# Hybrid RWKV-7 / MoBA / MoE layer: group norm from a centred V inside the attention's loop, probabilities divided by their sums ahead of the turn

## The reference, cut to what matters

```python
# RWKV-7 branch, 8 heads of 64: state recurrence over tokens, then per head and token
sa = einsum('bhij,bhj->bhi', state, a_t)
state = state * w_t + sa[..., None] * b_t + v_t[..., None] * k_t
y_t = einsum('bhij,bhj->bhi', state, r_t)
...
mean = jnp.mean(y, axis=-1); var = jnp.mean(jnp.square(y - mean), axis=-1)
yn = (y - mean) * lax.rsqrt(var + LN_X_EPS) * lnx_g + lnx_b
bonus = jnp.sum(r * k * r_k, axis=-1) * v
out_a = (yn + bonus) * g
# attention branch, 8 heads of 64, here equal to causal attention over 512 tokens
q, k = rope(rms_norm(q)), rope(rms_norm(k))
p = softmax(q @ k.T * 64 ** -0.5 + mask); out_b = p @ v
# merge
merged = sigmoid(g_a) * (out_a @ w_br_rwkv) + sigmoid(g_b) * (out_b @ w_br_moba)
x = x + gate1 * (merged @ w_out)
```

## Time and profile before

| | us |
|---|---|
| median of three runs | 1057.08 |
| the profiled execution | 1062.92 |
| its span | 1061.0 |
| TensorE busy in the span | 1019.7 (96%) |
| Vector engine busy | 532.0 (50%) |
| ScalarE busy | 314.6 (30%) |
| POOL busy | 133.2 (13%) |
| mean granted TensorE clock | 0.995 of full |

### The profile page before, as it was taken

How to read it: one execution, slowest core, us unless ns; L and a number is a source line. 1 busy time by engine, 2 the same in 40 slices (tenths; PEclk the granted TensorE clock), 3 DMA queues, 4 the chain that set the end, 5 groups by cost and what they waited for, 6 DMA issues and landing times.

```text
span 1061.0 us, 19592 instructions
## 1 busy us (share of the span) xinstructions
PE 1019.7 (96%) x8618; PEld 663.9 (63%) x8618; DVE 532.0 (50%) x789; ACT 314.6 (30%) x546; POOL 133.2 (13%) x156
## 2 busy tenths in 40 slices
PE   8999999999898999999999999999999999999998
PEld 6777899999895778878788434444434434344343
DVE  4668842256547656575665524443334334343344
ACT  4467742033336761321333111111111111111110
POOL 0000000464945700000000100000000000000000
PEclk9999999999999999999999999999999999999999
DMA  9632021000003057467488899999999999999994
GB/s 388 230 116 113 3 80 43 12 5 5 4 4 159 8 178 241 156 219 237 168 363 335 305 409 419 428 425 427 427 426 426 427 426 428 428 425 419 415 415 158
DMA packets 42982, 273.29 MB, mean 258 GB/s; under 512 B 8032, under 2 KB 8176, under 8 KB 28688
## 3 DMA queue, kind: packets, MB, share of 16 engines
q1 hardware_dynamic: 39488, 264.42, 62.0%
q0 software_dynamic: 2400, 4.28, 1.2%
q10 hardware_dynamic: 1008, 3.31, 0.8%
HBM read 272.00 MB, written 4.19 MB: 260 GB/s over the span
## 4 chain that ended last, share of the span: by engine, by line
PE 80%; DMA 9%; DVE 5%; ACT 4%; issue 2%; SPq 0%; DVEq 0%; ACTq 0%; POOLq 0%
PE banks L1704 29%; PE banks L2198 18%; PE banks L2212 9%; DMA w_qkv<-in_w 4%; DMA w_tok<-in_w 3%; PE banks L2236 2%; DMA ring<-in_w_mix 2%; PE banks L2237 2%; PE banks L2204 2%; PE banks L2184 1%; PE banks L1864 1%; PE banks L1862 1%; PE banks L1877 1%; ACT xT L913 1%; DVE tokm_r L1084 1%
## 5 line engine op out<-in xcount | busy, mean ns | idle before, releaser
L1583 DVE TENSOR_TENSOR hid<-banks,silu_a 64x512 f32<-64x512 f32 x32 | 22.2, 693 | 197.8 <-ACT silu_a L918 197.8
L2212 PE MATMUL banks<-w_ring,hidT 128*64 128x512 f32 x512 | 116.8, 598 | 1.1 <-ACT hidT L922 1.1
L1570 DVE SCALAR_TENSOR_TENSOR mod<-banks,row_weight,mod 64x512 f32<-64x512 f32 x64 | 47.9, 748 | 70.3 <-PE banks L2212 69.3
L918 ACT ACTIVATE silu_a<-banks 64x512 f32<-64x512 f32 x32 | 18.9, 591 | 206.3 <-PE banks L2199 206.3
L2198 PE MATMUL banks<-w_tok,xT 128*64 128x512 f32 x176 | 78.3, 595 | 0.3 <-DMA w_ring<-in_w 0.3
L2199 PE MATMUL banks<-w_ring,xT 128*64 128x512 f32 x176 | 78.3, 596 | 0.0
L1577 DVE TENSOR_TENSOR x<-x,banks 128x1024 f32<-128x1024 f32 x60 | 71.8, 1219 | 12.6 <-PE banks L2237 12.2
L2199 PE MATMUL banks<-w_tok,xT 128*64 128x512 f32 x176 | 77.9, 595 | 0.0
L2212 PEld LDWEIGHTS banks<-w_ring,hidT 128*64 128x64 f32 x512 | 34.3, 136 | 67.1 <-issue 65.8
L1704 PE MATMUL banks<-x_r,ring_r 128*128 128x512 f32 x192 | 75.0, 391 | 0.6 <-DVE tokm_r L1084 0.6
L2198 PE MATMUL banks<-w_ab,xT 128*64 128x512 f32 x160 | 70.7, 595 | 3.7 <-DMA w_tok<-in_w 3.7
(11 more groups left out here) (394 smaller groups left out, 2314.5 us busy)
## 6 DMA issues: line engine op xcount, KB each, us to landing
w_ring<-in_w SPq DMA_DIRECT2D x42, 2048.0 KB, 25.3
w_tok<-in_w SPq DMA_DIRECT2D x16, 2048.0 KB, 26.2
ada_buf<-in_w_ada SPq DMA_DIRECT2D x64, 256.0 KB, 3.5
w_ab<-in_w SPq DMA_DIRECT2D x8, 2048.0 KB, 25.8
w_qkv<-in_w SPq DMA_DIRECT2D x7, 2048.0 KB, 29.5
w_tok<-in_w SPq DMA_DIRECT2D x24, 512.0 KB, 16.5
w_ring<-in_w SPq DMA_DIRECT2D x24, 512.0 KB, 17.0
w_ring<-in_w SPq DMA_DIRECT2D x10, 1024.0 KB, 15.1
```

Of the source, the lines that this page charges most:

```text
L1570: dve.scalar_tensor_tensor(dst[:, 512 * n:512 * n + 512], bank[5][SLOTS * n:SLOTS * n + SLOTS, :], weight_of(e), gate2[:, n, :], ALU.mult, ...
L1583: dve.tensor_tensor(hid[:, :], bank[3][SLOTS:P, :], silu_a[:, :], ALU.mult).then_inc(hid_v, 1)
L2212: mm = pe.matmul(bank[5][SLOTS * n:SLOTS * n + SLOTS, :], hidT[:, k, :], w2[:, k, 512 * n:512 * n + 512], start=(k == 0), stop=(k == 3))
```

## The change

- A constant "centre" (identity minus the head mean) is added, and turn() makes V's rows with a product with it in place of a transpose. y comes out centred, so the head sums of y and the subtraction go.
- ScalarE squares y from PSUM beside its copy. Four products with 32 columns of `head_ones` put the sums of squares of all four tiles into one bank, ScalarE takes one root of it, the Vector engine one reciprocal in two halves. spread_inverse(ct), two products by 512 columns, spreads a tile's rows over its channels again; normed(ct) on the Vector engine multiplies y with lnx_g and this. lnx_b is added to the bonus by POOL beforehand, so POOL has four passes a tile.
- q and k are turned in the order of the head pairs: four sets before the loop, four in it (units 3 to 6). Gate products 0 and 1 come ahead of the loop, 2 and 3 in units 0 and 7, the spreads in units 1, 2, 8, 9.
- The probabilities are scaled by the inverse sum on the Vector engine (normalised(u)) before turn_probs(u), which now waits for that; the spreading of the inverse sums, its copy and its product go. PROB has three buffers. TensorE's order is scores(u+2), turn_probs(u), weighted(u-1); the Vector engine's is row_max(u+2), normalised(u), y_att(u-1); ScalarE is one unit further ahead with exps.
- The cuts of the branch weights move to units 10 to 13.

```diff
+    parts["centre"] = eye - same / HD
...
+        gn_rows, gn_inverse = mod[:, 0, :], mod[:, 1, :]
+        PROB = [flat[:, at:at + 1024].rearrange("p (o n) -> p o n", o=2) for at in (4096, 5120, 0)]
+        y_squares = ada_buf[:, 1:5, :]
+        QK_ORDER = (0, 4, 1, 5, 2, 6, 3, 7)
+        QK_BANK = (4, 6, 5, 7, 7, 7, 7, 7)
+        QK_AT = {3: 4, 4: 5, 5: 6, 6: 7}
+        GATE_BANK = (4, 5, 7, 7)
+        GATE_AT = {0: 2, 7: 3}
+        SPREAD_GN_AT = {1: 0, 2: 1, 8: 2, 9: 3}
-        BR_CUT_AT = (4, 6, 8, 10)
+        BR_CUT_AT = (10, 11, 12, 13)
...
 ScalarE
+                    act.activation(y_squares[:, :, CH * at:CH * at + CH], bank[2 * n + 1][:, 0:256].rearrange("p (c t) -> p c t", c=CT), ACT.Square)
                     act.activation(ahat[:, :, CH * at:CH * at + CH], ..., ACT.Copy).then_inc(out_a, 1)
+            for i in range(3):
+                turned_qk(i)
+            act.wait_ge(gn_mm, GN_MM["squares"])
+            act.activation(gn_rows, bank[3][:, :], ACT.Sqrt, bias=eps_x, scale=1.0 / HD).then_inc(gn_a, 1)
+            turned_qk(3)
+            act.activation(small[:, 57:58], one, ACT.Exp)
...
             exps(0)
+            gate_out(0)
+            gate_out(1)
+            exps(1)
             for u in range(NUNIT):
-                if u + 1 < NUNIT:
-                    exps(u + 1)
+                if u + 2 < NUNIT:
+                    exps(u + 2)
                 turned_probs(u)
-                if u:
-                    sums_out(u - 1)
+                if u in GATE_AT:
+                    gate_out(GATE_AT[u])
+                if u in QK_AT:
+                    turned_qk(QK_AT[u])
...
 POOL
             for ct in range(CT):
-                seq(pool.tensor_tensor(y_, y_, xs[ct], ALU.mult))
-                seq(pool.tensor_scalar(y_, y_, col["lnx_g"][:, c1], col["lnx_b"][:, c1], ALU.mult, ALU.add))
+                pool.wait_ge(gn_v, 2 + ct + 1)
+                pool.wait_ge(gn_a, 1 + ct + 1)
                 seq(pool.tensor_tensor(y_, y_, zr[:, 8 + ct, :], ALU.add))
...
 Vector engine
+            def norm_inverse(half):
+                c = slice(256 * half, 256 * half + 256)
+                dve.wait_ge(gn_a, 1)
+                dve.reciprocal(gn_inverse[:, c], gn_rows[:, c]).then_inc(gn_v, 1)
+            def normed(ct):
+                dve.wait_ge(gn_mm, GN_MM[f"spread{ct}"])
+                dve.scalar_tensor_tensor(ahat[:, ct, :], ahat[:, ct, :], col["lnx_g"][:, ct:ct + 1], bank[7][:, :], ALU.mult, ALU.mult).then_inc(gn_v, 1)
+            def normalised(u):
+                at, n = 8 * (u % 4), P * (tile_of(u) + 1)
                 dve.wait_ge(exp_a, 2 * u + 2)
-                dve.reciprocal(stat[:, at + 6:at + 8], stat[:, at + 4:at + 6]).then_inc(rsum_v, 1)
+                seq(dve.reciprocal(stat[:, at + 6:at + 8], stat[:, at + 4:at + 6]))
+                for odd in range(2):
+                    prob = PROB[u % 3][:, odd, 0:n]
+                    dve.tensor_scalar(prob, prob, stat[:, at + 6 + odd:at + 7 + odd], None, ALU.mult).then_inc(rsum_v, 1)
...
+            row_max(0)
             norm_inverse(0)
+            row_max(1)
             norm_inverse(1)
-            row_max(0)
-            row_max(1)
             for u in range(NUNIT):
-                inverse_sum(u)
                 if u + 2 < NUNIT:
                     row_max(u + 2)
-                if u in NORM_AT:
-                    norm_inverse(2 + NORM_AT.index(u))
+                normalised(u)
                 if u - 1 in BR_CUT_AT:
                     cut_branch_weights(0, BR_CUT_AT.index(u - 1))
                 if u:
                     y_att(u - 1)
+                if u in SPREAD_GN_AT:
+                    normed(SPREAD_GN_AT[u])
...
 TensorE
-                for i, src in enumerate((zr[:, 8 + ct, :], xp[1], xp[4], ahat[:, ct, :])):
+                pe.matmul(bank[7][:, 0:P], zr[:, 8 + ct, P * t:P * t + P], const("centre"), start=True, stop=True)
+                for i, src in ((1, xp[1]), (2, xp[4]), (3, ahat[:, ct, :])):
...
+            turn_qk(0)
+            turn_qk(1)
+            pe.wait_ge(out_a, NCH - 1)
+            turn_qk(2)
             pe.wait_ge(out_a, NCH)
             for ct in range(CT):
+                mm = pe.matmul(bank[3][32 * ct:32 * ct + 32, :], const("head_ones")[:, 48:80], y_squares[:, ct, :], start=True, stop=True)
+            mm.then_inc(gn_mm, 1)
+            turn_qk(3)
...
             def turn_probs(u):
-                pe.wait_ge(exp_a, 2 * u + 2)
+                pe.wait_ge(rsum_v, 2 * u + 2)
...
             scores(0)
+            pe.wait_ge(gn_a, 1)
             scores(1)
+            pe.wait_ge(s_lora_w, 48)
+            output_gate(0)
+            pe.wait_ge(qk_a, 3)
+            output_gate(1)
+            pe.wait_ge(gn_a, 3)
             for u in range(NUNIT):
-                turn_probs(u)
                 if u + 2 < NUNIT:
                     scores(u + 2)
+                turn_probs(u)
                 if u:
                     weighted(u - 1)
+                (u = 0: output_gate(2); 1, 2: spread_inverse(0), (1); 3 to 6: turn_qk(4) to (7); 7: output_gate(3); 8, 9: spread_inverse(2), (3))
```

More of the change, by code:

```diff
@@ L766, in _, with turned_qk @@
[L766 to L775, removed]
+            def turned_qk(i):
+                j = QK_ORDER[i]
+                act.wait_ge(qk_mm, i + 1)
+                act.activation((qT, kT)[j // 4][:, j % 4, :], bank[QK_BANK[i]][:, :], ACT.Copy, scale=(1.0 if j // 4 else -HD ** -0.5)).then_inc(qk_a, 1)
@@ L1973, in _, with turn_qk, output_gate @@
                         outputs(1, n)
+            def turn_qk(i):
+                j = QK_ORDER[i]
+                c0 = W * (j // 4) + P * (j % 4)
+                for t in range(TT):
+                    if i < 2:
+                        pe.wait_ge(rope_done, 2 * t + 1 + j // 4)
+                    mm = pe.transpose(bank[QK_BANK[i]][:, P * t:P * t + P], qkv[:, t, c0:c0 + P], ident)
+                mm.then_inc(qk_mm, 1)
+            def output_gate(ct):
+                pe.matmul(bank[GATE_BANK[ct]][:, :], lora_g[:, P * ct:P * ct + P], zr[:, 13, :], start=True, stop=True).then_inc(gn_mm, 1)
@@ L1975, in _, with spread_inverse @@
+            def spread_inverse(ct):
+                rows = slice(HD * (ct // 2), HD * (ct // 2) + HD)
+                for h in range(2):
+                    c = 32 * ct + 16 * h
+                    mm = pe.matmul(bank[7][HD * h:HD * h + HD, :], ident[rows, c:c + 1].to_broadcast([HD, HD]), gn_inverse[rows, :], start=True, stop=True)
+                mm.then_inc(gn_mm, 1)
[3 more added lines that the diff above has]
+            turn_qk(2)
             pe.wait_ge(out_a, NCH)
@@ L1976, in _ @@
             for ct in range(CT):
-                pe.matmul(bank[ct][:, :], const("head_ones"), ahat[:, ct, :], start=True, stop=True).then_inc(gn_mm, 1)
-            pe.wait_ge(s_lora_w, 48)
-            for ct in range(CT):
-                pe.matmul(bank[4 + ct][:, :], lora_g[:, P * ct:P * ct + P], zr[:, 13, :], start=True, stop=True).then_inc(gn_mm, 1)
-            for ct in range(CT):
-                pe.wait_ge(gn_v, CT + ct + 1)
-                pe.matmul(bank[ct][:, :], const("head_ones"), xs[ct], start=True, stop=True).then_inc(gn_mm, 1)
@@ L1986, in _ @@
-            for j in range(8):
-                if j >= 4:
-                    pe.wait_ge(qk_a, j - 3)
-                else:
-                    pe.wait_ge(gn_a, j + 1)
-                for t in range(TT):
-                    if j in (0, 4):
-                        pe.wait_ge(rope_done, 2 * t + 1 + j // 4)
-                    c0 = W * (j // 4) + P * (j % 4)
-                    mm = pe.transpose(bank[4 + j % 4][:, P * t:P * t + P], qkv[:, t, c0:c0 + P], ident)
-                mm.then_inc(qk_mm, 1)
@@ L2027, in weighted @@
                 p, i = u // TT, tile_of(u)
-                pe.wait_ge(rsum_v, u + 1)
-                if u:
-                    pe.wait_ge(rs_out, u)
-                for odd in range(2):
-                    at = 8 * (u % 4) + 6 + odd
-                    mm = pe.matmul(bank[7][HD * odd:HD * odd + HD, 0:P], stat[:, at:at + 1].to_broadcast([P, HD]), ident, start=True, stop=True)
-                mm.then_inc(rs_mm, 1)
                 pe.wait_ge(pt_a, u + 1)
```

84 lines of the change are left out of this document (49 added, 35 removed).

## The result

| | before | after |
|---|---|---|
| median | 1056.91 us (1056.73 to 1061.21, 4 runs) | 1106.32 us (1105.23 to 1107.97, 4 runs) |
| the profiled execution, its span | 1062.92, 1061.0 | 1106.41, 1104.6 |
| from scores(2) to the merge's first product | 338.06 to 380.52: 42.5 | 325.99 to 422.31: 96.3 |
| granted clock in that stretch | 0.96 | 0.66 |

The ratio is 1.0434, 95% interval 1.0402 to 1.0466. The forecast was 1078 with a range to 1096: sign and place were right, the size was not.

The account below looks back on a forecast made before the run. The attention was taken as bound by TensorE. Terms -12.9 + 25.6 - 0.4 + 2.5 = +14.8, with +6 for the clock about +21, gave 1084 profiled; with the median 5.8 lower, 1078, range 1065 to 1096.

Parts of the forecast that it names:

- Centring: In 16 turn() calls, one of four turns becomes a product with the constant "centre": +2.5 us, low end +1.8.
- Ahead of the loop: Between recurrence and attention, head sums, sums of squares and half the gate products leave the path: scores(2) earlier, -12.9 us.
- The loop at full clock: Attention loop: TensorE and Vector engine take turns, and moved products add in series: 68.1 against 42.46 us, +25.6.
- scaling's mean far from 0.33: Sign of being wrong: the probability scalings in the loop, priced 0.43 to 0.23 us by width, average far from 0.33.
- TensorE's clock: In the loop, a pause per unit, one in three followed by a clock fall, five falls: +6 us.
- The rule cited there: A matmul engine idling briefly between groups has its clock swing; by it the clock is low in much of the loop.
- the clock stays low: Rival: half clock over three quarters of TensorE's 41 us in the loop, +30 in place of +6: 1102; chance 0.12.
- POOL and the Vector engine: Rival: they slow each other, the fast scaling is lost in half of the units: +2.6 us, inside the range.
- Behind the loop: After the loop, cut_item(0) starts without the last sums_out and the gate products lose most of their wait: -0.4 us.

Follow-up runs that it names:

- e3: The kernel before with only V's turn made a product with the centring constant, head sums and subtraction kept: 1063.4 us, ratio 1.0015.
- e9: The changed kernel with POOL's group-norm passes put behind the attention loop and six identity products in TensorE's pause ahead of each turn: 1113.2 us, ratio 1.0477.
- e6: The changed kernel with POOL's group-norm passes put behind the whole attention loop: 1134.9 us, ratio 1.0711.
- e2: The changed kernel with six products of the identity put into TensorE's pause ahead of each turn_probs(u): 1087.1 us, ratio 1.0232.
- e5: The changed kernel with the Vector engine dividing unit u+1, not u, behind the row maximum of unit u+2: 1065.2 us, ratio 1.0032.
- e8: The changed kernel with the division one unit ahead and written as a tensor_tensor in place of tensor_scalar: 1064.8 us, ratio 1.0022.
- e1: The changed kernel with normalised(u) ahead of row_max(u+2) on the Vector engine: 1085.5 us, ratio 1.0210.
- e13: e11 with the group norm's two reciprocals moved, one behind the row maxima of units 0 and 1, one behind normalised(1): 1058.8 us, ratio 0.9971.
- e11: e5 with POOL's memset of mod put behind the last unit: 1061.6 us, ratio 0.9994.

## Why the prediction was right and wrong

In spans: forecast 1061.0 + 20.8 = 1081.8, measured 1104.6, so 22.8 short. By its steps:

- *Centring*, +2.5: trace 1.8, e3 +2 within its interval. Right.
- *Ahead of the loop*: with the centring, scores(2) at 338.06 + 2.5 - 12.9 = 327.7; it started at 325.99, so 1.7 better.
- *The loop at full clock*, 68.1: the alternation came as described, and e9 has it at 71.9 with neither low clock nor POOL. Of the 3.8 more, 0.8 are the added products that outlast a pause; the rest was not assigned. Right within that. Only the divisions were sized too short even without POOL: the forecast's "scaling's mean far from 0.33" as a sign of being wrong came true, with 0.50 us over the four widths in the change and 0.38 in e9.
- *TensorE's clock*, +6: **this is the step that failed**, by 11: it measures 17.2 us (e6 to e9; 16.8 from the change to e2). Both are what filling the pauses gives back. The forecast counted falls, one for three pauses and 1.7 us each, from pauses that stood alone among busy stretches. In this loop the pauses follow one another, and the granted clock stays at its lower level, 1.2 GHz, for 28 us and more. The rule cited there (the Trainium skill, TensorE: Matmul & The Clock Gate, A second HAM failure mode: psum-queue depth-cycling) was set aside for the count of nine single pauses. Now the trace agrees with it: granted 0.66 over 96 us, and 0.98 to 1.00 once the pauses hold work. The rival "the clock stays low" had the right mechanism, at a chance of 0.12. That its 1102 comes near 1106 is partly luck: it put the clock at 30 us where 17 were measured, and left out POOL's 7.
- *POOL and the Vector engine*, left out of the sum and put at 2.6 as a rival: 7.3 to 7.7 us. The rival took away only the fast form of the division, 0.69 us in place of 0.43; but a pair that meets POOL's passes grew by 0.3 to 1.3 us in the change, and by 3.3 around the memset in e5. The trace of before had the sign of it, unread: of its four cuts of the branch weights, a Vector pass with two inputs in SBUF, the two that start inside a POOL pass are longer (1.67 and 1.53) than the two that don't (1.22, the fourth at 371.78 in the earlier trace rows). The Vector engine's timeline of before, then POOL's:

```profile
353.88 1.67 DVE L1341 TENSOR_TENSOR ring_r<-ring,mid_r 128x1024 fp32r<-128x1024 f32 x1
361.37 1.53 DVE L1341 TENSOR_TENSOR ring_r<-ring,mid_r 128x1024 fp32r<-128x1024 f32 x1
365.61 1.22 DVE L1341 TENSOR_TENSOR ring_r<-ring,mid_r 128x1024 fp32r<-128x1024 f32 x1
```
```profile
353.21 1.26 POOL L987 TENSOR_TENSOR ahat<-ahat,mod 128x512 f32<-128x512 f32 x1
354.57 1.62 POOL L988 TENSOR_SCALAR ahat<-ahat,cols 128x512 f32<-128x512 f32 x1
...
360.55 1.27 POOL L992 TENSOR_TENSOR mid_r<-ahat,zr_r 128x512 fp32r<-128x512 f32 x1
361.88 3.53 POOL L994 MEMSET mod<- 128x4096 f32 x1
```

The first cut ends 1.08 us behind the pass at 353.21, the second 1.08 behind the pass at 360.55, and the memset that runs beside the second's rest adds nothing, as in e8. POOL's pass at 354.57 waited in its turn: it takes 1.62 us, where the same pass takes 0.77 elsewhere (346.84).

- *Behind the loop*: 680.1 forecast from the merge's first product to the end (1061.0 - 380.52 - 0.4), 682.3 measured; the merge's first products still ran at the low clock (granted 0.53 at 424 to 428).

Sum: -1.7 + 3.8 + 11.2 + 7.3 + 2.2 = 22.8. The other 5.5 of the 28.3 us are the base: the median of before lay 5.8 below its profiled execution and the forecast took that off, while the profiled execution of after is at its own median (1106.41 and 1106.32). On the later chips the kernel before had medians of 1061 to 1062.

## What to carry to other kernels

Put what TensorE waits for a step early, where its input is ready, and ahead of whatever itself waits for TensorE: here moving one operation by one unit in one queue was worth 4% of the time (1106.3 to 1065.2) with the same arithmetic, and half of that was lost where it still stood behind y_att (e1). When a pause recurs in every step of a TensorE loop, price the lower clock as a state and not fall by fall from single pauses. In this loop TensorE is busy 65.7 us, where the same work takes 43.8 at a clock of 1.00 (e13), and 17 us of those 22 show in the loop. A Vector pass of these forms (a column scaling, or two inputs, from SBUF) that is put on the path can wait for the POOL pass that it meets, so add up to that pass's length. The row minima, which read PSUM, show no such growth (942 ns for 768 columns with and without POOL).

## What the hardware did that was not expected

- A pair of fp32 tensor_scalar took 4.10 us around a memset of POOL of 3.61 us (e5) and 0.77 without it (e11); the tensor_tensor form took 0.76 inside the memset (e8). Beside POOL's other passes both forms take two to three times as long (2.06 against 0.75; 2.45 against 1.03), while most of POOL's passes gain little (1.46 for 1.26) and one in the kernel before took 1.62 for 0.77.
- Six products of an identity with itself in each pause, 27 us of useless work, made the changed kernel 19 us faster (1106.3 to 1087.1; ratios 1.043 and 1.023).
